# The RWKV mixer's sums over a head's channels: one whole-array product with a block-diagonal matrix in place of two 64x64 products

## What is computed

```python
kk = kk / jnp.maximum(jnp.sqrt(jnp.sum(kk * kk, -1, keepdims=True)), 1e-12)
...
yc = y - jnp.mean(y, -1, keepdims=True)
y = yc * lax.rsqrt(jnp.mean(yc * yc, -1, keepdims=True) + GN_EPS)
...
bonus = jnp.sum(rf * kh * r_k, -1, keepdims=True) * vh
```

## Time and profile before

| What | us |
|---|---|
| median of 3 runs (lowest, highest) | 3052.31 (3051.36, 3053.95) |
| time of the profiled execution | 3045.93 |
| its span, first to last instruction | 3043.8 |
| TensorE busy in the span | 2724.1 |
| VectorE busy in the span | 1763.7 |
| ScalarE busy in the span | 1090.1 |

### The profile page before, as it was taken

The page is one execution under the profiler, slowest core; times in us unless marked ns, Lnnn a source line. Parts: engine busy times, 40 slices in busy tenths (PEclk is TensorE's granted clock), DMA queues, the critical chain, the costliest instruction groups (busy, mean ns, idle before and its releaser), DMA issues. The chain is left out here.

```text
span 3043.8 us, 69421 instructions
## 1 busy us (share of the span) xinstructions
PE 2724.1 (89%) x28140; PEld 2005.8 (66%) x28140; DVE 1763.7 (58%) x3756; ACT 1090.1 (36%) x2589; POOL 531.9 (17%) x508
## 2 busy tenths in 40 slices
PE   6999999999999999958989899999998399999970
PEld 6888888888888888845555556554554255555540
DVE  1666666666666666656767675872233654544428
ACT  2233333333333333324545454541222033333326
POOL 0000000000000000001000000001111266556625
PEclk9999999999999999969999999999998699999985
DMA  6122222122222222222010101005443489999537
GB/s 204 37 39 39 39 39 39 39 39 39 39 39 39 39 39 39 64 56 89 1 41 2 41 1 38 1 1 168 162 157 130 194 266 337 368 319 303 145 66 246
DMA packets 336905, 303.11 MB, mean 100 GB/s; under 512 B 236654, under 2 KB 291982, under 8 KB 322192
## 3 DMA queue, kind: packets, MB, share of 16 engines
q1 hardware_dynamic: 318016, 248.31, 27.0%
q0 software_dynamic: 18576, 50.36, 6.8%
HBM read 208.64 MB, written 85.47 MB: 97 GB/s over the span
## 5 line engine op out<-in xcount | busy, mean ns | idle before, releaser
L800 PE MATMUL mx_bank<-mx_xT,mx_w_in 128*128 128x128 f32 x5168 | 644.9, 280 | 17.2 <-DVEq L263 13.7
L800 PEld LDWEIGHTS mx_bank<-mx_xT,mx_w_in 128*128 128x128 f32 x5168 | 599.3, 192 | 60.8 <-issue 36.2
L1501 PE MATMUL at_bank<-pl_kT,pl_qT 128*128 128x512 f32 (+5 forms) x656 | 288.5, 526 | 2.3 <-issue 2.3
L2229 POOL DMA_INDIRECT ex_x<-scr_hx,ex_plan x192 | 228.7, 1191 | 106.9 <-issue 56.1
L1463 ACT ACTIVATE at_PQ<-at_bank,at_nms 128x512 f32<-128x512 f32 (+5 forms) x328 | 193.3, 595 | 118.7 <-DVE at_nms L1602 115.7
L696 ACT ACTIVATE mx_pr<-mx_bank 128x256 f32<-128x256 f32 (+1 forms) x68 | 36.7, 540 | 553.3 <-PE mx_bank L800 471.7
L1598 DVE TENSOR_REDUCE at_mx<-at_bank 128x1 f32<-128x512 f32 (+5 forms) x328 | 189.0, 576 | 43.0 <-PE at_bank L1501 38.3
L1533 PEld LDWEIGHTS at_bank<-at_PT,at_vals 128*64 128x64 f32 (+1 forms) x2208 | 117.4, 136 | 145.9 <-issue 81.1
L1513 PE MATMUL at_bank<-pl_at_ident,at_PQ 128*128 128x128 f32 x1104 | 183.7, 281 | 15.9 <-ACT at_PQ L1463 9.8
L2298 PE MATMUL ex_gate<-pl_wg,ex_xT 128*64 x768 | 176.4, 383 | 21.9 <-issue 19.8
L651 POOL TENSOR_TENSOR mx_AR<-mx_u,mx_ep 128x512 f32<-128x512 f32 x17 | 20.1, 1179 | 998.8 <-DVE mx_kh L1140 998.8
(11 more groups left out here) (346 smaller groups left out, 5391.3 us busy)
## 6 DMA issues: line engine op xcount, KB each, us to landing
pl_wg<-in_w_eg SPq DMA_DIRECT2D x32, 1024.0 KB, 12.3
pl_wu<-in_w_eu SPq DMA_DIRECT2D x32, 1024.0 KB, 16.3
pl_wd<-in_w_ed SPq DMA_DIRECT2D x32, 1024.0 KB, 9.6
mx_x<-in_x SPq DMA_DIRECT2D x76, 128.0 KB, 3.9
scr_acc<-ro_blank SPq DMA_DIRECT2D x19, 512.0 KB, 6.2
pl_ro_x<-in_x SPq DMA_DIRECT2D x17, 512.0 KB, 5.5
scr_hx<-ro_h SPq DMA_DIRECT2D x17, 512.0 KB, 2.7
scr_acc<-ro_ha SPq DMA_DIRECT2D x17, 512.0 KB, 3.2
```

The lines of the kernel that those rows point to most:

```text
L800: ins = pe.matmul(dst, w_in[:, k, col:col + n], xT[:, k, :], start=(k == 0), stop=(k == KC - 1))
L1501: t.mark(pe.matmul(bank[n % SB][:, 0:wd], qT[h][keys(h), j * P:(j + 1) * P], kT[h][keys(h), k0 * P:k0 * P + wd], start=True, stop=True), f ...
L2229: x_in[s].go(g.indirect_dma_start(x[s][:, k, :], None, rows, bass.IndirectOffsetOnAxis(ap=idx[:, at:at + 1], axis=0)))
```

## The change

`by_halves` goes, and `by_heads` takes its place in all four calls: one product over all 128 rows and columns of the array. Its stationary operand is a 128x128 matrix with two diagonal blocks of 64x64 (ones in `whole_heads[:, 0]`, 1/64 in `whole_heads[:, 1]`) and zeros beside them, so each output row still sums its own head alone. The full matrices were in DRAM already, as the input `cst`, of which the kernel before loads the diagonal blocks; one DMA of 128 KB (128 rows of 1 KB) now loads two of them whole, and the group `consts` counts ten DMAs in place of nine. `bones` and `bmean` in `cst` stay loaded, and are not read any more.

```diff
+        whole_heads = sb("whole_heads", [P, 2, P])
...
-        early, consts = Dmas(nc, ctx, "mx_early", 2), Dmas(nc, ctx, "mx_consts", 9)
+        early, consts = Dmas(nc, ctx, "mx_early", 2), Dmas(nc, ctx, "mx_consts", 10)
...
             consts.go(sp.dma_start(w_g[:], io["w_g"]))
+            consts.go(sp.dma_start(whole_heads[:], io["cst"].rearrange("p (a n) -> p a n", a=7)[:, 0:2, :]))
...
-            def by_halves(dst, w, src):
-
-                for r in range(2):
-                    hs = slice(64 * r, 64 * r + 64)
-                    ins = pe.matmul(dst[hs], w[hs], src[hs], start=True, stop=True)
-                return ins
+            def by_heads(dst, k, src):
+
+                return pe.matmul(dst[:, :], whole_heads[:, k, :], src, start=True, stop=True)
...
-                t.mark(by_halves(bank[7], bones, t1[:].rearrange("p a n -> p (a n)")), "kk_norm")
+                t.mark(by_heads(bank[7], 0, t1[:].rearrange("p a n -> p (a n)")), "kk_norm")
...
-                t.mark(by_halves(bank[5], bones, t1[:].rearrange("p a n -> p (a n)")), "bonus_sum")
+                t.mark(by_heads(bank[5], 0, t1[:].rearrange("p a n -> p (a n)")), "bonus_sum")
...
-                t.mark(by_halves(bank[4], bmean, ys[:].rearrange("p a n -> p (a n)")), "y_mean")
+                t.mark(by_heads(bank[4], 1, ys[:].rearrange("p a n -> p (a n)")), "y_mean")
...
-                t.mark(by_halves(bank[7], bmean, yq[:].rearrange("p a n -> p (a n)")), "y_var")
+                t.mark(by_heads(bank[7], 1, yq[:].rearrange("p a n -> p (a n)")), "y_var")
```

## The result

The changed kernel takes 3059.26 us (median of 12 runs, 3056.55 to 3062.43), the kernel before 3051.97 us (12 runs). The ratio is 1.0027, with a 95% interval from 1.0018 to 1.0035: slower by 8 us by the ratio, by 7.3 us between the two medians. The forecast was 3053.7 us and no difference that can be told. The profiled execution took 3060.7 us, with a span of 3058.7.

A forecast was written before the change was run, and what follows sets the result against it. ScalarE was taken to set a steady pass's first leg, TensorE the second. DMA 0.4, kk_norm 0.75, pass 1 -0.1 and last passes 0.3 gave +1.35 on 3052.31, so 3053.7 us; range 3049.5 to 3057.5.

The forecast's parts named there:

- The chain of the pass: Steady pass: ScalarE sets about 15.8 us up to kk_norm, TensorE about 60.3 us from there to stage b's end.
- The sizes on TensorE: At the four calls: y_mean and y_var together save about 0.65 us a pass, kk_norm costs 0.05 more, bonus_sum no difference.
- So stage c gives 0: In ScalarE's leg: the 0.65 us saved at y_mean and y_var becomes waiting and idle time, gaining 0.
- the sum: Whole kernel: DMA 0.4, kk_norm 0.75, pass 1 -0.1, last two passes 0.3, together +1.35 us.
- its slower rival: Last two passes: the clock stays at its lower level, 9.3 us more, up to 3063 us; chance 4%.
- `kk_norm`'s bare load: At kk_norm in the second leg: an unhidden weight load, 0.05 us more in 15 passes, +0.75 us; pass 1 -0.1.
- The new DMA: At the start: loading whole_heads delays the constants by 0.33 to 0.60 us, taken as 0.4, paid once.
- The last two passes: From 1284 us: four calls with someone waiting pay 0.05 us each, or 0.10 at the lower clock, +0.3 us.
- The terms named for the range: Likeliest case, whole kernel: from -1 (kk_norm cheaper by 0.05, DMA 0.33) to about +2.5 (DMA 0.6, last passes 0.8).
- those of the rivals: Whole kernel: faster 6%, 1% and 1%; slower 4% and 2% beyond 6.1 us; the forecast itself had 85%.

The follow-up runs named there:

- the second order: ScalarE's kk_sq, ckv_sq and kpe_part moved ahead of kh_gain: 3031.67 us on the kernel before, 3029.81 us on the changed kernel.
- Stage c alone: Against the changed kernel, kk_norm and bonus_sum back to two 64x64 products, only y_mean and y_var whole-array: 3060.16 us, ratio 1.0026.
- the longer ScalarE leg: The kernel before plus one ScalarE activation of unread result ahead of kk_sq: 3068.28 us, ratio 1.0052.
- the filled kernels: The changed kernel with useless TensorE work added: y_var done twice, 3056.07 us; line 828's sixteen small products done twice, 3054.60 us.
- the DMA alone: Against the changed kernel, all four calls back to two 64x64 products, new DMA and count of ten kept: 3051.27 us, ratio 1.0004.

## Why the prediction was wrong

**The chain of the pass: right.** Two legs, ScalarE's from `y` to `kk_sq` and TensorE's from `kk_norm` on. Stage c gave nothing directly; the idle time came to 1.80 us where 1.8 to 2.0 was forecast, and a pass without a low clock is 76.14 us. The kernels that shorten ScalarE's leg show it: the second order took 1.4 us off each pass. A new wait of 0.16 us at line 948 (0.1 to 0.2 forecast) is there as well.

**The sizes on TensorE: right.** `y_mean` and `y_var` each take 0.86 to the next product, `kk_norm` 1.05 (1.06 forecast), and stage c saves 0.62 a pass (0.65 forecast). `bonus_sum` costs no difference: from `kk_norm` to it 15.37 us in place of 15.41, although `kk_norm` costs 0.05 more, and from it to the next `kk_norm` 60.77 in place of 60.68, so what is saved ahead of it is lost behind it. The halves do run side by side: in the kernel before their MATMULs start 7 ns apart, and there was nothing to halve. The rule of the Trainium skill (page "TensorEngine Tiling (Array Packing)", section "Restrictions and Gotchas") that different row tiles cannot be in one PSUM bank at the same time was not borne out by any trace here.

**"So stage c gives 0": this is the step that failed.** The prediction let the saved 0.46 us become idle time and priced that at nothing. But with more idle time ahead of `kk_norm` (1.80 us in place of 1.34) the granted clock was lower behind it in 4 of 15 passes, and the same 120 MATMULs took about 1.5 us more there, in the leg that nothing covers. The whole distance to `bonus_sum` grew by 1.6 us, and 4 x 1.6 = 6.4 us, where the sum had 0. Stage c alone and the longer ScalarE leg show it from two sides, and the filled kernels show its absence. The prediction did name the clock as its slower rival, at 4%, but looked for it in the last two passes, where the clock was low already, and not at the place where it had itself forecast idle time to grow.

**`kk_norm`'s bare load: right.** A steady pass without a low clock is 0.05 us longer, 0.75 us in 15. Pass 1 is 0.05 us shorter, where 0.1 was forecast.

**The new DMA: about right, and not to be measured.** The constants came 0.60 us later, the upper of the two prices. The start as a whole varies more than that from one execution to the next. The first `kk_norm` is at 81.9, 85.1, 83.8, 85.2, 84.0 and 84.7 us in the profiled executions without the DMA, and at 86.6, 84.2, 85.9, 88.4, 84.2, 87.1, 83.5, 86.9 and 84.9 in those with it: means of 84.1 and 85.7. Single kernels of either group differ by 3 to 5 us, so the 1.6 us between the means is an estimate and not clear of chance. Of the 4.7 us between the two executions that the study began with, some 3 are then chance. 2.85 us of the 4.7 are the low clock behind the idle time that ends at 71.72 us (6.69 us for what took 3.84). Five kernels without the DMA show it too, with 5.2 to 6.4 us for the same 32 MATMULs. The kernel with the DMA alone has a ratio of 1.0004.

**The last two passes: not told apart.** From `kk_norm` of pass 17 to the end, the span of the changed kernel is 3.1 us longer (1748.0 against 1744.9), against 0.3 in the sum. Kernels without any whole-array product vary there by 4 us among each other (1744.9 before, 1746.9 with the DMA alone, 1749.1 with the longer ScalarE leg). How much of the 3.1 is the change's stays open.

The sum that the runs support is 1.6 (start) + 0.75 + 6.4 = 8.8 us, an estimate with the last two passes left open, against 8.2 by the ratio.

**Two slips in the prediction's arithmetic.** The terms named for the range add up to -0.2 us at the low end (0.33 - 0.75 - 0.1 + 0.3) and +2.05 us at the high end (0.6 + 0.75 - 0.1 + 0.8), not to -1 and +2.5. The chance of the forecast and those of the rivals add up to 101%. Neither decides anything here: the 6.4 us that were missing lie outside all of these terms.

## What to carry to other kernels

Where a change saves time on the engine with the clock that can fall, ask first where the saved time goes. If it becomes idle time ahead of a wait, look for how long the longest idle time in the loop will be then, and for what the engine has to do right behind it; a saving in a covered leg can cost more than it saves. Then shorten the leg that covers it: here moving ScalarE's steps was worth 19 to 20 us, and the cheaper product paid only in a kernel where its saving was not covered. And compare the length of the same stretch in every pass, not the mean over all of them.

## What the runs showed of the hardware

- The granted clock fell behind an idle time of 1.79 to 1.86 us in 4 or 5 of 15 passes that looked alike (three kernels), and in none of 15 with 1.34 to 1.37 us (four kernels) or 0.94 us (one), each in one execution. Elsewhere in a pass TensorE had only two waits of 0.48 us and, in some kernels, one of 0.16. No run has an idle time between 1.37 and 1.79 us. In the changed kernel a pass with the fall has TensorE's operations ahead of it at the same moments as its neighbours, to 0.03 us, while those of VectorE and GpSimd differ by up to 1.3 us between passes, hit or not. So which passes are hit isn't explained here.
- Behind an idle time of 3.45 us at the start the granted clock was at its lower level in 14 of 15 profiled executions, and 32 MATMULs took 5.2 to 6.7 us there in place of 3.84.
- Dividing the array anew costs about 0.10 us each way plus the first weight load that is no longer hidden (0.10 us for 128 columns, 0.05 for 64), an estimate from the earlier trace rows; with it the forecast for stage c was 0.65 us a pass, and 0.62 was measured. Two 64x64 products of 512 columns side by side took 1.01 us up to the next whole-array product, one whole-array product 0.86.
- Two products on different rows of the array wrote the same PSUM bank at the same time without slowing each other: four MATMULs in 1.01 us, the two halves 7 ns apart, where 0.43 is the time of one (half of the 0.86 above).
